# Where a vector-times-matrix product is streamed: 160 of its 192 weight chunks beside the first feed-forward block, none beside the latent attention and the second output projection

## The reference

```
ada = jax.nn.silu(c) @ w_ada[l] + b_ada[l]                      # 2048 x 12288 weights, one row
shift_m, scale_m, gate_m, shift_f, scale_f, gate_f = split(ada, 6)
h = rms_norm_2(x, g_pre_mix[l]) * (1.0 + scale_m) + shift_m
z = h @ w_in[l]                                                 # then latent attention + linear attention
o = jnp.concatenate([o_mla, o_gla], axis=-1) @ w_out[l]         # second output projection
x = x + gate_m * rms_norm_2(o, g_post_mix[l])
h = rms_norm_2(x, g_pre_ffn[l]) * (1.0 + scale_f) + shift_f
f = (jax.nn.silu(h @ w_ffn_gate[l]) * (h @ w_ffn_up[l])) @ w_ffn_down[l]
x = x + gate_f * rms_norm_2(f, g_post_ffn[l])
```

## Time and profile before

| | us |
|---|---|
| median of 3 timed runs | 2579.02 |
| profiled execution, its own time | 2581.83 |
| its span in the trace | 2579.7 |
| TensorE busy | 2405.9 (93%) |
| VectorE busy | 1609.6 (62%) |
| ScalarE busy | 1128.4 (44%) |
| GpSimd busy | 328.8 (13%) |

### The profile page before, as it was taken

The page is one execution under the profiler, slowest core; times in us unless marked ns, Lnnn a source line. Parts: engine busy times, 40 slices in busy tenths (PEclk is TensorE's granted clock), DMA queues, the critical chain, the costliest instruction groups (busy, mean ns, idle before and its releaser), DMA issues.

```text
span 2579.7 us, 37706 instructions
## 1 busy us (share of the span) xinstructions
PE 2405.9 (93%) x15624; PEld 2158.2 (84%) x15624; DVE 1609.6 (62%) x2135; ACT 1128.4 (44%) x1737; POOL 328.8 (13%) x178
## 2 busy tenths in 40 slices
PE   6999878989999999999979998796999999999997
PEld 5998766779999889999858786574999988999985
DVE  3347995468877557778555454887555555554444
ACT  3335554544444334444435463435344344444442
POOL 0002210223233322333310000000000000000000
PEclk9898985989999999999989899697999999999998
DMA  7743220546776877777745462694666676655552
GB/s 179 254 148 104 89 66 1 173 168 233 244 244 230 277 239 243 241 253 248 255 152 160 143 189 94 224 377 167 225 219 217 216 231 228 223 184 184 184 195 82
DMA packets 137770, 502.02 MB, mean 195 GB/s; under 512 B 15312, under 2 KB 15312, under 8 KB 137344
## 3 DMA queue, kind: packets, MB, share of 16 engines
q1 hardware_dynamic: 136368, 494.37, 57.1%
q0 software_dynamic: 1232, 5.24, 1.3%
HBM read 494.31 MB, written 5.24 MB: 194 GB/s over the span
## 4 chain that ended last, share of the span: by engine, by line
PE 81%; DVE 12%; ACT 3%; DMA 2%; issue 2%; POOL 1%; SPq 0%; ACTq 0%; DVEq 0%
PE bank L581 75%; DVE conv_y L1641 4%; DVE w_lo L1477 2%; DMA raw<-weights 1%; DVE ada_acc L1461 1%; PE bank L553 1%; ACT w_hi L1045 1%; PE bank L747 1%; PE bank L712 0%; PE bank L618 0%; DVE wide L1495 0%; DVE x L1999 0%; PE bank L656 0%; DVE wide L1997 0%; DVE scores L1589 0%
## 5 line engine op out<-in xcount | busy, mean ns | idle before, releaser
L1477 DVE TENSOR_TENSOR w_lo<-raw,w_hi 128x1024 fp32r<-128x1024 f32 (+1 forms) x618 | 805.1, 1316 | 565.9 <-ACT w_hi L1045 565.1
L581 PE MATMUL bank<-h_hi,w_hi 128*128 128x256 f32 x3472 | 995.9, 287 | 8.9 <-DVE w_lo L1477 8.8
L581 PE MATMUL bank<-h_lo,w_hi 128*128 128x256 f32 x3472 | 990.5, 285 | 0.0
L581 PE MATMUL bank<-h_hi,w_lo 128*128 128x256 f32 x3472 | 989.8, 285 | 0.0
L1045 ACT ACTIVATE w_hi<-raw 128x1024 fp32r<-128x1024 f32 (+1 forms) x737 | 759.3, 1052 | 519.7 <-PE bank L581 468.8
L581 PEld LDWEIGHTS bank<-h_hi,w_hi 128*128 128x128 f32 x3472 | 674.1, 194 | 16.6 <-DVE w_lo L1477 11.7
L581 PEld LDWEIGHTS bank<-h_lo,w_hi 128*128 128x128 f32 x3472 | 674.2, 194 | 0.2
L581 PEld LDWEIGHTS bank<-h_hi,w_lo 128*128 128x128 f32 x3472 | 673.7, 194 | 0.0
L2058 POOL TENSOR_TENSOR w_lo<-raw,w_hi 128x1024 fp32r<-128x1024 f32 (+1 forms) x119 | 305.6, 2568 | 933.4 <-ACT w_hi L1045 933.4
L1461 DVE SCALAR_TENSOR_TENSOR ada_acc<-raw,stat,ada_acc 128x1024 f32<-128x1024 f32 x180 | 285.9, 1589 | 1.6
L581 PE MATMUL bank<-w_hi,ff_hi 128*128 128x512 f32 x704 | 275.9, 392 | 1.9 <-POOL w_lo L2058 1.0
(11 more groups left out here) (291 smaller groups left out, 2014.2 us busy)
## 6 DMA issues: line engine op xcount, KB each, us to landing
raw<-weights SPq DMA_DIRECT2D x924, 512.0 KB, 4.4
bias_rows<-table POOLq DMA_DIRECT2D x1, 3072.0 KB, 36.2
raw<-weights SPq DMA_DIRECT2D x5, 504.0 KB, 4.3
x<-x SPq DMA_DIRECT2D x2, 1024.0 KB, 5.8
bias<-bias_rows POOLq DMA_DIRECT2D x1, 2048.0 KB, 17.0
out<-x SPq DMA_DIRECT2D x8, 256.0 KB, 2.0
lasting<-params SPq DMA_DIRECT2D x1, 550.0 KB, 7.8
raw<-weights SPq DMA_DIRECT2D x1, 488.0 KB, 4.2
```

Of the source, the lines that this page charges most:

```text
L581: t = e.matmul(out, s, m, start=opens and first and q == 0, stop=closes and last and q == 2)
L1477: e.tensor_tensor(w_lo[:, slot, 0:widths[i]], raw[:, i % RAW_SLOTS, 0:widths[i]], w_hi[:, slot, 0:widths[i]].bitcast(F32), ALU.subtract).t ...
```

## The change

Both lines of the plan that place ada chunks are moved. The rate beside the first feed-forward block is 0.58 and goes on until 32 chunks are left, so that 160 stand there; three of these fall in behind the last `down1` group (before, one). No ada chunk stands between the latent attention's weights and the second feed-forward block, whose 32 chunks stay as they were. The setting `p.open = False` starts a fresh chunk where before the ada chunks did; the first piece of `out2` now shares a chunk with the last piece of `mla_v`. The guard that protects the memory which `ada_acc` shares with the latent projections moves to the sums that now come after them (10 and 11). The numbers of split chunks, of ada chunks, of chunks taken by GpSimd and of matmuls stay as they are.

```
-ADA_BESIDE_LATENT = 24
...
         p.project(("out1", n), "w_out", 512 * n, 512)
-        p.ada_until(3 * 2 * KD, 0.35)
+        p.ada_until(2 * KD, 0.58)
...
-    for _ in range(ADA_BESIDE_LATENT):
-        p.put_ada()
-    p.ada_until(2 * KD, 1.3)
     for n in range(4):
         p.project(("out2", n), "w_out_2", 512 * n, 512, order=MIX_ORDER)
-    p.finish_ada()
+    p.open = False
     p.ada_until(0, 0.2)
...
-                    if m in (6, 7):
+                    if m in (10, 11):
...
                 next(linear, None)
-                rests_until(min(ada_first + ADA_BESIDE_LATENT * (u + 1) // NM, ada_first + ADA_BESIDE_LATENT - 1))
```

## The result

The median of the changed kernel was 2581.53 us (20 runs, 2579.76 to 2591.34) against 2578.82 us for the kernel before, measured beside it (20 runs, 2576.24 to 2581.32): a ratio of 1.0016, 95% interval 1.001 to 1.0023. The change made the kernel 0.16% slower where 0.8% was forecast: 2.7 us where 20.7 were expected. The profiled execution took 2580.93 us (span 2578.8).

The account below looks back on a forecast made before the run. TensorE bounds the feed-forward tiles, VectorE the latent attention with low-clock TensorE next. Costs 45.3 less gains 24.6 give +20.7 us on the profiled 2581.83, so 2602.5, median 2600; range 2571 to 2613.

Parts of the forecast that it names:

- What goes from the latent attention: Latent attention: VectorE's ada chunks leave, TensorE at its low clock bounds next; gain 14 us, ends 9.5 and 30.1.
- Rival 2: Latent attention: TensorE goes at full clock, gain 30.1 us for 14, net +4.6, 2583.6; chance 0.14.
- What goes from `out2`: `out2`: earlier start 3.1 us, three reductions inside it 5.0, waits for chunks' rests 2.5; together 10.6 us gained.
- What the first feed-forward block gets: First feed-forward block: added TensorE time from four more reductions, late chunks, port collisions and a `down1` wait; 41.4 us.
- reductions: First feed-forward block: nine sums finish instead of five, 4 x 1.68 = 6.7 us of TensorE.
- lookahead: Feed-forward tiles: at 14 of 88, one split chunk ahead; TensorE waits 1.7 us for GpSimd's chunk, 23.8 us.
- collisions: Feed-forward tiles: VectorE's rest starts just after GpSimd's, TensorE 0.97 us late, at 11 tiles for 3; 7.8 us.
- `down1`: First feed-forward block, second half: after the second `down1` group TensorE waits for GpSimd's chunk, 3.1 us.
- VectorE's total: Feed-forward tiles: VectorE's busy time per half rises from 205.2 to 246 of 257 us and fits; nothing added.
- rival 3: Feed-forward tiles: VectorE saturates, delays add up, TensorE follows; 10 us more for each half, 2620; chance 0.10.
- The start of the second block: After the last `down1` group: no chunk of the next projection is prepared, TensorE starts 3.9 us late.
- Rival 1: First feed-forward block: the thin lookahead doesn't bite, 23.8 + 3.1 us of costs go, net -6.2, 2573; chance 0.16.

Follow-up runs that it names:

- one-column kernel: Kernel before, VectorE's additions of the 24 ada chunks beside the latent attention cut to one column, except each sum's first chunk: 2558.35 us against 2577.40.
- kernel with more matmuls: Kernel before, two further unread matmuls in each latent attention step from the fourth on, VectorE's work whole: 2577.97 us against 2577.40.
- deeper lookahead: Changed kernel, three split chunks prepared ahead in the first feed-forward block and `out2`: 2543.24 us; on the plan of the kernel before: 2569.17 us.

## Why the prediction was wrong, point by point

- **What bounds the kernel** (the tiles hide nothing more without cost, the latent attention waits for VectorE): right.
- **"What goes from the latent attention": the step that failed.** "At the clock as it is, the gain lies between 9.5 and 12.3 ... I take 14." It gave 25.5 in one profile, 21.0 in the other. The step subtracted TensorE's busy time, most of it at the lower clock level, from the stage and took little more than the rest for the gain. But that busy time depended on the clock, which had fallen while TensorE stood waiting 1.68 and 1.96 of 4 us for the work that the change removes. The one-column kernel shows the gain without any other part of the change (21.4), the kernel with more matmuls that the clock alone gives next to none of it (1.0). VectorE's work there was also read too high: the view of the earlier trace rows has 23 additions because it takes in the one at 1664.99, behind the attention, so 28.9 us stood on VectorE and not 30.1. Rival 2 named this outcome and got a chance of 0.14. Against it stood the first attention's 0.50 at 29.93 of 30 busy. That row shows that small matmuls without a gap can stay at the lower level; the second profile of the changed kernel shows 13.7 us of the same. What it didn't show is how long such a stretch lasts in this stage.
- **The rule of the Trainium skill** (TensorE: Matmul & The Clock Gate, Part 1) says that activity releases the throttle. In this stage the traces agree: 1.00 in the first profile after VectorE's work went, and 1.00 with two more matmuls a step. The stretches at 0.50 with TensorE busy 4.00 of 4 show that a busy row alone does not say which level is granted.
- **"What goes from `out2`"**: 10.6 forecast, 14.9 measured (3.0 + 11.9). The start (3.1), the three reductions (5.0) and the waits (2.5) came as worked out. Not counted was that the first 12 matmuls ran at half clock before and at full clock now: 5.23 - 2.72 = 2.5 us. It is the same slip about the clock. Of the 1.8 us left, 1.0 lie between `out2`'s last matmul and the second block (33.1 us before, 32.1 now), where the fourth reduction stood that was to give nothing; 0.8 are not assigned.
- **"What the first feed-forward block gets"**: reductions, lookahead, collisions and `down1` were 6.7 + 23.8 + 7.8 + 3.1 = 41.4; the block grew by 39.5. Read from the starts of TensorE's matmuls, the reductions came to 6.8 and the 14 late chunks to 22.7 (1.64 each, one of 1.33). The collisions were over-counted: the tiles have 8 for 3 before, one of them small, and that is 4.6 us more and not 7.8. The wait after the second `down1` group was 1.3 as shown, not 3.1, and the `down1` groups together gave 1.9. That makes 36.0; the other 3.5 us are small delays, about one of them from a longer stretch at half clock under the first tiles (4.8 us for 3.0). So the sum came near 39.5 in part by luck: two terms were too high, and this one was not in it. The deeper lookahead brought the block to 774.0 us, 1.8 under the kernel before, with the reductions still in it.
- **VectorE's total**: 10 us a half was set at nothing, rightly; rival 3 fell. Its busy time came to 237.6 us for a half's tiles, not 246, since the ada additions took 1.46 us on average and not 1.94, while the rests went from 1.70 to 2.05.
- **The start of the second block**: 3.9 forecast, 3.5 measured.
- **Rival 1** (the lookahead doesn't bite) fell: each of its 14 places was late.
- **The whole**: with 21 and 14.9 in place of 14 and 10.6, the same sum gives 45.3 - 35.9 = 9.4 over before; with 25.5, 4.9; the executions show 7.2 and 3.3, the medians 2.7.

## What to carry to other kernels

- TensorE's busy time at half clock is no floor. Before taking it for the next bound, look at what it did when its clock fell: if it stood waiting for the very work that is removed, work the stage out at full clock too and put the forecast between the two.
- A lookahead counted in plan positions shrinks without notice when chunks are strewn in that another engine alone uses. Counted in what the bounding engine needs, the same plan went from 0.16% slower to 1.4% faster than the kernel before; alone, the new plan gave nothing and the deeper lookahead 0.4%.
- Two waits can hide behind one another (a late chunk, then a port collision): undoing the one paid 12 us where 28 were expected, and only the step beyond paid the rest.

## What the runs showed of the hardware that was not expected

- The same instructions took 125.9 or 130.4 us in two executions of one kernel, with TensorE's clock at the lower level for 10.2 or 20.5 us of them. I found nothing in the program that says which it will be.
- That clock fell 5.4 to 5.8 us after the attention's first scores in ten profiles, with VectorE's work in place or not, and in the first profile of the changed kernel it did not.
- Two idle-filling matmuls of 128x256 in each step of the attention kept the clock at 1.00 through some 48 us in which it had been at 0.50 to 0.56, at no cost and with no gain (+0.6 us in one execution, within what executions of one kernel differ by): VectorE was the bound at both levels.
- A one-column addition on VectorE still took 213 ns, against 745 for 512 columns and 1278 for 1024: the cost beyond the first 213 is 1.04 ns for each column.
